# A top-k threshold search on raw float bits, split anew between VectorE, ScalarE and GpSimd

## What is computed

```
isc = relu(einsum('bqhd,bsd->bqhs', qib, k_idx))
isc = einsum('bqh,bqhs->bqs', wib, isc) * idx_scale
isc = where(admissible, isc, -inf)
top_val, top_idx = lax.top_k(isc, 256)
c_sel = c_kv[bidx, top_idx]
...
s = s - slopes * abs(tpos - top_idx)
s = where(sel_ok, s, -inf); p = softmax(s)
```

## Time and profile before

| | us |
|---|---|
| median of 3 runs | 3640.78 (3635.86 to 3640.91) |
| the profiled execution, by its own time | 3632.74 |
| its span in the profile | 3630.6 |
| halves stage in the profile | 1966.2 to 2484.8 |
| latent stage | 2484.8 to 2621.6 |

### The profile page before, as it was taken

One profiled execution on the slowest core, in us unless ns is written; L12 is line 12 of the kernel. 1 busy time (PEld: TensorE's weight loads), 2 busy tenths in 40 slices (PEclk: granted clock), 3 DMA queues, 4 the chain that ended last, 5 costly groups with the idle time before them and its releaser, 6 DMA issues. The chain is left out here.

```text
span 3630.6 us, 90143 instructions
## 1 busy us (share of the span) xinstructions
PE 3319.4 (91%) x36861; PEld 2889.6 (80%) x36861; DVE 2132.6 (59%) x5023; ACT 1897.3 (52%) x3756; POOL 817.9 (23%) x900
## 2 busy tenths in 40 slices
PE   5899999989888888996997999998789999999899
PEld 5777899978777776885765898897678888888787
DVE  7100100018788984331199999997967777787332
ACT  5122211126677773221386766756468888888311
POOL 3222200001377771001101533521510000000000
PEclk9999999999899999998999999998899999999999
DMA  5333421149513214356321436425663333331432
GB/s 197 110 116 116 148 67 62 48 112 229 148 38 84 72 51 144 107 160 216 104 59 49 138 113 187 138 91 172 208 178 96 84 84 84 96 84 51 154 113 86
DMA packets 368041, 416.90 MB, mean 115 GB/s; under 512 B 51744, under 2 KB 272800, under 8 KB 366368
## 3 DMA queue, kind: packets, MB, share of 16 engines
q1 hardware_dynamic: 302880, 318.55, 30.4%
q10 hardware_dynamic: 64768, 92.81, 7.1%
HBM read 247.21 MB, written 164.10 MB: 113 GB/s over the span
## 5 line engine op out<-in xcount | busy, mean ns | idle before, releaser
L1433 PE MATMUL s_o<-s_v,s_pT 128*64 128x65 f32 (+1 forms) x13056 | 435.9, 224 | 6.5 <-issue 6.5
L230 PE MATMUL s_acc<-s_wh,s_hT 128*128 128x256 f32 (+1 forms) x1408 | 430.1, 305 | 8.6 <-ACT s_parts L658 4.6
L1433 PEld LDWEIGHTS s_o<-s_v,s_pT 128*64 128x64 f32 x13056 | 401.4, 138 | 42.9 <-issue 22.0
L232 PE MATMUL s_acc<-s_wh,s_hT 128*128 128x256 f32 (+1 forms) x1408 | 429.2, 305 | 0.0
L231 PE MATMUL s_acc<-s_wl,s_hT 128*128 128x256 f32 (+1 forms) x1408 | 429.1, 305 | 0.0
L230 PE MATMUL s_acc<-s_hT,s_wh 128*128 128x512 f32 x880 | 349.6, 397 | 55.8 <-DVE s_wl L334 25.7
L1596 ACT ACTIVATE s_probs<-s_probs,s_nmx 128x512 f32<-128x512 f32 (+3 forms) x640 | 388.7, 662 | 12.2 <-DVE s_nmx L1661 12.2
L1645 DVE CUSTOM_DVE_ANT_0 s_probs<-s_s,s_scores 128x512 f32<-128x512 f32 (+3 forms) x640 | 364.7, 607 | 10.8 <-issue 6.9
L2380 DVE TENSOR_SCALAR_CACHE_REDUCE s_scratch<-s_scores,s_thr 128x384 uint8<-128x384 f32 (+4 forms) x320 | 365.3, 1209 | 1.1
L231 PE MATMUL s_acc<-s_hT,s_wh 128*128 128x512 f32 x880 | 347.5, 395 | 0.0
L232 PE MATMUL s_acc<-s_hT,s_wl 128*128 128x512 f32 x880 | 345.7, 393 | 0.0
(11 more groups left out here) (278 smaller groups left out, 7153.7 us busy)
## 6 DMA issues: line engine op xcount, KB each, us to landing
fm<-s_parts ACTq DMA_DIRECT2D x120, 512.0 KB, 2.8
s_y<-y SPq DMA_DIRECT2D x32, 640.0 KB, 5.8
y<-s_g SPq DMA_DIRECT2D x18, 1024.0 KB, 5.9
s_q<-fm SPq DMA_DIRECT2D x32, 512.0 KB, 6.5
kc<-s_parts SPq DMA_DIRECT2D x32, 512.0 KB, 3.5
s_w<-in_o_fm SPq DMA_DIRECT2D x25, 512.0 KB, 4.5
s_w<-in_o_w_in SPq DMA_DIRECT2D x12, 1024.0 KB, 5.3
s_qh<-fm SPq DMA_DIRECT2D x42, 256.0 KB, 3.3
```

The source lines that it names most:

```text
L230: nc.tensor.matmul(out, sh, mh, start=(j == 0), stop=False)
L232: ins = nc.tensor.matmul(out, sl, mh, start=False, stop=(j == n - 1))
L1433: last = nc.tensor.matmul(o_ps[half * HD:(half + 1) * HD, 0:w], pT[half][:, x0:x0 + HD], v[:, g.u.kbs[g.a + x], vc:vc + w], start=(g.first ...
```

## The change

- The search now works on the bits of the float itself. `best` starts at zero with all bits flipped, and each round's candidate is `best` exclusive-or one mask of a table, which can be compared as a float at once. `as_float`, the shift and the `bit` tile leave the round. After the rounds `as_key` turns the result back into the sortable key.
- `ND` is 9 and `NA` 5: ScalarE counts the block of width 1536 too.
- In the halves stage ScalarE empties a wide event once, in full, and GpSimd makes the rounded high part by a copy before the low part.
- `EARLY` is 10: the blocks of widths 1152 to 1536 are chosen in the halves stage too, by a new `choose_wide`, since the scratch holds 1024 columns. The latent stage keeps 4 blocks.
- `after` is 31, and the recounts come at 4 a slot.
- In the latent stage the means and normalizations of tiles 8 to 15 stand ahead of the first pair, and low parts stand midway in both pairs.

```
-    ND = 10
+    ND = 9
-    EARLY = 6
-    PER = 7
+    EARLY = 10
+    PER = 4
+    MASKS = [0xFFFFFFFF] + [1 << n for n in range(30, -1, -1)]
...
+                    nc.gpsimd.tensor_copy(parts[b][:, 0, :], parts[b][:, 1, :].bitcast(F32)).then_inc(hi_made, 1)
+                    pool.wait_ge(hi_made, f + 1)
                     nc.gpsimd.tensor_tensor(parts[b][:, 1, :], parts[b][:, 1, :].bitcast(F32),
...
-                        nc.scalar.mul(parts[b][:, 0, :], acc[e % 4][:], scale)
                         nc.scalar.mul(parts[b][:, 1, :].bitcast(F32), acc[e % 4][:], scale).then_inc(raw_made, 1)
...
+    def as_key(self, dve, src):
+        v = self.nc.vector
+        self.link(dve, v.tensor_scalar(self.flip[:], src[:], 31, SIGN, ALU.arith_shift_right, ALU.bitwise_or))
+        self.link(dve, v.tensor_tensor(src[:], src[:], self.flip[:], ALU.bitwise_xor))
...
-            self.link(dve, v.tensor_tensor(self.cand[:], self.best[:], self.bit[:], ALU.bitwise_or))
-            self.as_float(dve, self.cand)
+            self.link(dve, v.tensor_scalar(self.cand[:], self.best[:], self.MASKS[i], None, ALU.bitwise_xor))
...
-            v.tensor_scalar(self.bit[:], self.bit[:], 1, None, ALU.logical_shift_right)
...
+    def choose_wide(self, dve, n, even, rank):
+        v, L, H = self.nc.vector, self.width(n), PIECE
+        t = self.thr[:, n:n + 1].bitcast(F32)
+        room, room_left = self.room[:, n:n + 1], self.cnt[:, 0:1]
+        def rank_equal(x0, x1):
+            ev, rk = even[:, 0:x1 - x0], rank[:, 0:x1 - x0]
+            self.link(dve, v.tensor_scalar(ev, self.scores(n + self.B0)[:, x0:x1], t, None, ALU.is_equal))
+            self.link(dve, v.tensor_tensor_scan(out=rk, data0=ev, data1=ev, initial=0.0, op0=ALU.add, op1=ALU.max))
+        def keep(x0, x1, left):
+            sc_b, ev, rk = self.scores(n + self.B0)[:, x0:x1], even[:, 0:x1 - x0], rank[:, 0:x1 - x0]
+            self.link(dve, v.tensor_scalar(rk, rk, left, 2.0 ** -126, ALU.is_gt, ALU.mult))
+            self.link(dve, v.scalar_tensor_tensor(out=ev, in0=sc_b, scalar=t, in1=rk, op0=ALU.subtract, op1=ALU.is_lt))
+            self.link(dve, v.scalar_tensor_tensor(out=sc_b, in0=ev, scalar=MASKED,
+                                                  in1=self.neg_dist[:, S - L + x0:S - L + x1],
+                                                  op0=ALU.mult, op1=ALU.add))
+        rank_equal(H, L)
+        self.link(dve, v.tensor_tensor(room, room, rank[:, L - H - 1:L - H], ALU.add))
+        rank_equal(0, H)
+        self.link(dve, v.tensor_scalar(room, rank[:, H - 1:H], room, 0.5, ALU.add, ALU.mult))
+        self.link(dve, v.tensor_tensor(room_left, room, rank[:, H - 1:H], ALU.subtract))
+        keep(0, H, room)
+        rank_equal(H, L)
+        keep(H, L, room_left)
...
-                lead, span, after = 3, 2 * wide_slots + slots, 20
+                lead, span, after = 3, 2 * wide_slots + slots, 31
...
-                        due += min(search.NB, 2 * rest)
+                        due += min(search.NB, 4 * rest)
```

More of the change, by code:

```diff
@@ L2330, in __init__ @@
         self.neg_dist = sc.sb("neg_dist", [P, S])
-        self.best, self.bit, self.cand, self.flip, self.thr, self.enough = (
-            sc.sb(name, [P, self.NB], U32) for name in ("best", "bit", "cand", "flip", "thr", "enough"))
+        self.best, self.cand, self.flip, self.thr, self.enough = (
+            sc.sb(name, [P, self.NB], U32) for name in ("best", "cand", "flip", "thr", "enough"))
         self.high, self.low = (sc.sb(name, [P, self.NA], U32) for name in ("high", "low"))
@@ L2421, in settle @@
         best, cand = self.best[:, ND:NB], self.cand[:, ND:NB]
+        self.as_key(dve, self.best)
         v.tensor_copy(self.cand[:, 0:ND], self.best[:, 0:ND])
@@ L2919, in search_all @@
                     for n in range(search.EARLY):
-                        search.choose(dve, n, search.scratch[:, 0, :], search.scratch[:, 1, :])
+                        pick = search.choose if search.width(n) <= PIECE else search.choose_wide
+                        pick(dve, n, search.scratch[:, 0, :], search.scratch[:, 1, :])
                 project_halves(nc, hT, late_dram, a["o_fm"][QC:NFM], NFM - QC, scale[:, QC:NFM],
```

31 lines of the change are left out of this document (16 added, 15 removed).

## The result

The changed kernel takes 3647.3 us against 3635.9 for the kernel before on the same chip: a ratio of 1.0030, with a 95% interval of 1.0019 to 1.0040. It is slower, by 11 us (7 to 15). One of the nine timed runs of the changed kernel took 5846 us at a granted clock of 0.76, where all others have 0.97, and is left out of the ratio. The forecast was 3646, 5 us slower; the sum had the right sign and was 6 us short. That 3646 lies so near 3647.3 is luck: it stood on a median of 3640.8 from 3 runs of the kernel before, and nine runs give 3635.9.

A forecast was written before the change was run, and what follows sets the result against it. TensorE and VectorE were taken to end the halves stage level, VectorE to bound the latent stage. Halves 17.9 us longer minus latent 12.8 gave 5 us more: 3638 profiled, 3646 as median of runs, range 3633 to 3659.

The forecast's parts named there:

- The halves stage: Term for the halves stage: VectorE's choosing of wide blocks makes it end 17.9 us later (bounds 10 and 25).
- event 42: TensorE in the second half of the halves stage, 25 events before the last: reached 5 us earlier, at 2405.8.
- The rounds: Search rounds in the halves stage: VectorE's round 10.3 us, 2.5 less; sign counts fall due every 13.0 us.
- and not the reverse: Sign in the rounds: L2384 to L2384 about 13 us apart, VectorE waiting for ScalarE, not ScalarE for VectorE.
- ScalarE has 12% to spare: Rounds of the halves stage: ScalarE's counts and emptyings take 11.2 of 12.7 us wide, about 11.5 of 13.0 narrow.
- the rival: Halves stage: ScalarE bounds the rounds, TensorE waits, event 42 comes 5 us later than before; 3656 us, chance 0.2.
- The latent stage: Term for the latent stage: the next stage starts at 2608.8 instead of 2621.6, 12.8 us less (bounds 8 and 18).
- VectorE reaches `adjust` as before: Start of the latent stage: relative to the stage's start, VectorE comes to `adjust` at the same time as before.
- ScalarE takes the roots 5.7 us earlier: Latent stage: means no longer wait for a pair, so roots come 5.7 us earlier and TensorE's 3.5 us go.
- lasts 25.4: Latent stage: VectorE's pair of widths 1664 and 1792 takes 25.4 us, so the last pair starts at 2562.2.
- The third rival: Latent stage: GpSimd contention delays the last group's low parts another 4 us, only 8 us come back; 3651, chance 0.15.

The follow-up runs named there:

- e2: The changed kernel with `after` 39 instead of 31; ratio to the kernel before 1.0083.
- e8: The changed kernel with GpSimd's splits of weights in the halves stage in four pieces and `after` 39; ratio to the kernel before 1.0011.
- e6: The changed kernel with each split of weights in the halves stage made by four GpSimd copies and four subtractions; ratio to the kernel before 1.0035.
- e10: The kernel before with only the new form of the candidate and `as_key`; ratio to the kernel before 0.9990.
- e12: The kernel before with the new form of the candidate and `ND` 9, the fifth block on ScalarE; ratio to the kernel before 0.9975.
- e5: The changed kernel with GpSimd's subtraction in the latent stage done on one column of 512 only; one execution, 3639.0 us.
- e1: The changed kernel with the latent stage's low parts behind the pair's comparisons, not behind comparisons and running sums; ratio to the kernel before 1.0024.
- e4: The changed kernel with `EARLY` 8 and three pairs in the latent stage, low parts in the first two; ratio to the kernel before 1.0003.
- e7: The changed kernel with `EARLY` 9, low parts behind the comparisons and width 2048 chosen alone at the end; ratio to the kernel before 0.9998.

## Why the prediction held, and where it was off

**The halves stage.** Forecast 17.9 us longer, measured 18.5. In the frame of before (2.3 us less than the trace of after says) event 42 was emptied at 2406.7 for 2405.8, choosing started at 2421.4 for 2420.7, the six narrow blocks with the split took 36.2 for 36.4, the wide ones 9.7, 10.7, 11.7 and 12.7, 44.9 for 45.3, and VectorE ended at 2502.4 for 2502.4. A slope and a fixed part per instruction, read from two rows, priced 15 instructions of a new form to 0.4 us in 45. TensorE's last event was 2.2 us later than forecast, but hidden behind VectorE. That event 42 came within 0.9 us is partly luck. The sum let TensorE gain 5 us by losing its waits and the slower clock. In the first half's narrow events alone it lost 8 us less to them than before, and gave 6 of those back by matmuls that stand 5.3 ns further apart, a cost that the prediction did not have.

**The rounds.** Half right. The due numbers did set the mean, 13.4 us for 13.0. But I said that VectorE would wait for ScalarE "and not the reverse", and ScalarE waited 40.7 us. "ScalarE has 12% to spare" counted its load and left out that its five counts can't start before VectorE has ended the round: with 39 slots the chain of the two, lengthened by GpSimd, was the bound (e2, e8). How close under it 31 is, no run shows; the price of the rival, TensorE waiting ahead of event 42, was not paid. GpSimd's copies were 0.61 us for 0.6 (the lower bound of 0.5 is a quarter of 1.90, not half).

**The latent stage.** Forecast 12.8 us less, measured 8.1; this is the term that was mis-sized, though five executions of this code average 126.6 us, against 138.4 for three of the old, and that would be 11.8 less. In the profiled one three steps failed. "VectorE reaches `adjust` as before": it came 3.4 us later, behind a store that landed late and a stretch in which TensorE fell to the lower clock. ScalarE's idle time there, and TensorE's row of the stage's fourth 10 us (time, busy, granted clock, DMA share, GB/s):

```profile
2530.06 0.59 ACT L832 CAST s_parts<-s_acc 128x512 fp32r<-128x512 f32 x1 [1.82 <-DMA kc<-s_parts]
```

```profile
2535.65:2545.65 10.00, 9.78 (x63) 0.72 0.59 212
```

In e6, with the same code, those 10 us show 0.96 and 80 matmuls, and `adjust` comes at 36.1 us of the stage instead of 38.4. Most of the 3.4 us lies in the trace that the forecast was read from: its 35.0 us is the earliest of all fourteen, and e10 and e12, with the latent stage of before, have 37.3 and 37.5. "ScalarE takes the roots 5.7 us earlier" became 2.4, since ScalarE came to them 3.3 us later than in that trace. And the pair "lasts 25.4" took 28.6: e5 shows why. The low parts were done 6 us later than forecast, which is the sum of these (2.1, 3.2 and 0.6 in the second pair), and 4.7 us of it reached the stage's end. The prediction let a lateness of 3.7 us stand there (2573.1 to 2576.8); TensorE's stall was 7.3, and e1 shows that another place in VectorE's order removes it, for 2 us in the timed runs.

**The sum.** 18.5 - 8.1 + 2.3 ahead of the stages + 0.1 = 12.8 of the measured 12.9. The third rival ("the latent stage doesn't give", 10 us slower) described this execution best, and by the difference the timed runs too: 11 us, with the forecast's 5 below their interval. Only the absolute 3647.3 lies nearer to 3646 than to 3651, by the base that was 5 us too high.

**What the change bought.** Choosing starts 29.7 us sooner than before, of which some 13 come with nine blocks and the new rounds even at the old `after` (e12). It is spent on 45 us of wide blocks in a stage where VectorE and TensorE ended level, and that is the main cause of the loss: with eight early blocks and nothing else changed (e4) the kernel is level with before, and so with nine and sooner low parts (e7). Against e12 the rest of the change makes the halves stage 33 us longer and the latent one 11 to 13 shorter.

## What to carry to other kernels

Work that moves into a stage costs in full once its engine is the last to end; move only as much as the slack of that stage holds, block by block (here ten early blocks cost 11 us, eight and nine nothing). Where two engines hand a loop back and forth, reckon its period as the chain of both and not as the larger of two loads, and add what a third engine's instructions hold up at the hand-over (here up to 4.5 us at a time, 59 us in 32 rounds of e2); cut those instructions before raising the pace. When a wait is moved off one engine, see who stands in it next: the means had to go ahead for ScalarE and TensorE, and with nothing put between them and the normalizations VectorE stood for 10 us. And before an order is credited with microseconds read from one execution, look how far that stage differs between executions of the same code, and let the timed runs decide.

## What the runs showed of the hardware

- A GpSimd subtraction of 512 columns takes 1.28 us alone and 3.2 us beside VectorE's choice (e1); the same pair of VectorE's takes 20.6 us alone and 28.6 beside GpSimd (e5). Both lose.
- TensorE's narrow matmuls keep their distance for whole halves of the stage, 113.4 ns in some and 117.8 to 120.0 in others, at a granted clock of 1.00 and without a wait; with the wide ones (228.9 or 232.4 ns) that is up to 15 us of this stage. The granted clock doesn't tell them apart, a count of matmuls in a window does.
- The same code takes 125.3 to 128.7 us in the latent stage and 1008.9 to 1015.3 from there to the end, in single executions. The two tens of us behind the latent stage differ in the granted clock: 0.54 and 1.00 before, 0.50 and 0.59 in e4.
